# A two-block layer kernel on one core: the last expert's weights in another order and cut, and the last norm in two halves

## What is computed

```
probs = softmax(h @ w_router);  gate, idx = top_k(probs transposed, 64)   # 64 tokens per expert
xs = h[idx]
a = xs @ w_gate;  u = xs @ w_up             # [16, 64, 1024] x [16, 1024, 2048]
y = (silu(a) * u) @ w_down                  # [16, 64, 2048] x [16, 2048, 1024]
x = x + segment_sum(y * gate, idx)          # back to the 512 token rows
out = x * rsqrt(mean(x * x, columns) + 1e-6) * final_g
```

## Time and profile before

| | us |
|---|---|
| three runs, median | 2015.63 (2015.32 to 2016.61) |
| the profiled execution, its own time | 2017.26 |
| span of its trace, first to last instruction | 2015.9 |
| PE busy, of the span | 1843.2 (91%) |
| DVE busy | 594.0 (29%) |
| ACT busy | 284.5 (14%) |
| mean granted TensorE clock | 0.983 |
| moved by DMA | 589.86 MB |

### The profile page before, as it was taken

How to read it: one execution, slowest core, us unless ns; L and a number is a source line. 1 busy time by engine, 2 the same in 40 slices (tenths; PEclk the granted TensorE clock), 3 DMA queues, 4 the chain that set the end, 5 groups by cost and what they waited for, 6 DMA issues and landing times.

```text
span 2015.9 us, 20480 instructions
## 1 busy us (share of the span) xinstructions
PE 1843.2 (91%) x8850; PEld 842.5 (42%) x8850; DVE 594.0 (29%) x1103; ACT 284.5 (14%) x519; POOL 33.4 (2%) x44
## 2 busy tenths in 40 slices
PE   8999999999999989999998999888888889888886
PEld 4445788453333344567654333222222223222222
DVE  4478354341010147984323111111110111111112
ACT  3222100211101036231011000000000000000001
POOL 0000000010000010000000000000000000000000
PEclk9999999989999989999998999999999999999999
DMA  6221042369999942112458999999999999999996
GB/s 251 75 84 42 1 168 99 140 233 348 412 391 408 385 160 84 42 48 74 186 225 332 402 427 428 429 427 427 429 427 428 428 427 428 428 428 428 427 428 273
DMA packets 68542, 589.86 MB, mean 293 GB/s; under 512 B 5472, under 2 KB 6880, under 8 KB 37216
## 3 DMA queue, kind: packets, MB, share of 16 engines
q1 hardware_dynamic: 59904, 556.55, 67.1%
q10 hardware_dynamic: 4448, 17.28, 2.2%
q0 software_dynamic: 4096, 14.68, 2.1%
HBM read 575.91 MB, written 12.58 MB: 292 GB/s over the span
## 4 chain that ended last, share of the span: by engine, by line
PE 61%; DMA 32%; DVE 4%; issue 1%; ACT 1%; POOL 0%; ACTq 0%; DVEq 0%
PE ps L251 24%; DMA AR<-in_w_up 16%; PE ps L1241 11%; DMA AR<-in_w_down 9%; PE ps L2416 8%; DMA ring<-in_w_up 5%; PE ps L2442 5%; PE ps L787 3%; PE ps L2030 3%; PE ps L265 2%; PE ps L706 1%; PE ps L1920 1%; DMA ring<-in_exp_w_gate 1%; PE ps L2397 1%; PE ps L261 1%
## 5 line engine op out<-in xcount | busy, mean ns | idle before, releaser
L251 PE MATMUL ps<-AR,ring 128*128 128x512 f32 (+1 forms) x1160 | 383.1, 487 | 2.5 <-DVE AR L2246 2.4
L2556 DVE TENSOR_TENSOR XT<-XT,ps 128x512 f32<-128x512 f32 x128 | 81.9, 683 | 785.2 <-PE ps L2397 785.2
L251 PEld LDWEIGHTS ps<-AR,ring 128*128 128x128 f32 x1160 | 219.7, 190 | 155.8 <-issue 136.0
L2416 PE MATMUL ps<-ring,AR 128*64 128x512 f32 x1008 | 230.6, 601 | 48.4 <-DMA ring<-in_w_up 32.1
L2416 PE MATMUL ps<-AR 128*64 128x512 f32 x1040 | 235.5, 597 | 29.8 <-DMA AR<-in_w_up 23.8
L1241 PE MATMUL ps<-ring,AR 128*32 128x512 f32 x1536 | 249.5, 597 | 3.5 <-ACT AR L1389 1.9
L2416 PEld LDWEIGHTS ps<-ring,AR 128*64 128x64 f32 x1008 | 69.5, 137 | 201.9 <-issue 114.7
L2416 PEld LDWEIGHTS ps<-AR 128*64 128x64 f32 x1040 | 71.9, 137 | 189.5 <-issue 122.7
L251 PE MATMUL ps<-AR 128*128 128x256 f32 (+6 forms) x678 | 136.3, 346 | 6.7 <-DVE AR L1410 2.7
L1241 PE MATMUL ps<-AR 128*32 128x512 f32 x768 | 125.1, 595 | 0.0
L2442 PE MATMUL ps<-AR 128*64 128x512 f32 x528 | 117.9, 594 | 6.2 <-DMA AR<-in_w_down 6.2
(11 more groups left out here) (367 smaller groups left out, 1232.3 us busy)
## 6 DMA issues: line engine op xcount, KB each, us to landing
AR<-in_w_gate SPq DMA_DIRECT2D x33, 2048.0 KB, 35.0
AR<-in_w_down SPq DMA_DIRECT2D x33, 2048.0 KB, 35.4
ring<-in_w_up SPq DMA_DIRECT2D x32, 2048.0 KB, 35.4
AR<-in_w_up SPq DMA_DIRECT2D x32, 2048.0 KB, 35.0
ring<-in_w_gate SPq DMA_DIRECT2D x31, 2048.0 KB, 32.1
ring<-in_w_down SPq DMA_DIRECT2D x31, 2048.0 KB, 35.4
ring<-in_w_in SPq DMA_DIRECT2D x15, 2048.0 KB, 8.6
ring<-in_exp_w_gate SPq DMA_DIRECT2D x15, 2048.0 KB, 8.8
```

The lines of the kernel that those rows point to most:

```text
L251: x = PE.matmul(ps, l, r, start=i == 0, stop=i == len(pairs) - 1)
L2416: x = PE.matmul(GU[2 * m + f // 2][64 * (f % 2):64 * (f % 2) + 64, :], XS[n // 2 % 2][:, k * P + 64 * b:k * P + 64 * b + 64], w[:, kk_, f ...
L2556: DV.tensor_tensor(XK[:, o:o + T], XK[:, o:o + T], co_bank(i)[:, :], ALU.add).then_inc(d_co, 1)
```

## The change

Five edits, all at the last expert (number 15) and behind it.

1. The last expert's loads come as four gate parts, then four up parts, then the down parts; PE's loop follows. ACT's silu waits for the gate parts alone, and DVE waits for the up parts itself.
2. The last expert's down weights are cut by output columns: parts 0 and 1 hold columns 0 to 511 (1024 hidden rows each), parts 2 and 3 columns 512 to 1023. Each part is issued as two DMAs of 1 MB, whose contiguous runs are 2 KB. The second DMA of the last part has a semaphore of its own, so that PE can start on the first.
3. PE accumulates columns 0 to 511 in bank 4 and 512 to 1023 in bank 5. Even and odd hidden chunks go to the two partition halves, and the combine product with all 128 rows contracted adds the two. So there are 4 combine products of 128 rows for each column half: those of the first half stand between part 2 and part 3, those of the second after part 3. Eight banks are used so that few of them wait.
4. DVE adds the first column half, computes mean square/1024 + eps of it from ACT's sums, and multiplies the first half by `gn` while later work goes on. ACT squares the first half before it copies the second bank.
5. Behind the second half: ACT squares 512 columns of a row tile and takes the root with the first half's sum as bias; DVE takes the reciprocal and finishes the second half; ACT scales the first half by the reciprocal (`scaled`). The store of a tile waits for both. The last tile is stored as two halves, as before, the second column half first.

The diff, cut to this:

```diff
-        for e in range(16):
+        for e in range(15):
             ...
+        for m, (name, w) in enumerate((("cg", "w_gate_2"), ("cu", "w_up_2"))):
+            for c in range(4):
+                load(f"{name}15.{c}", runs(A[w][15], 256 * c, 2), e_gu, 120 + 4 * m + c + 1)
+        for c in range(4):
+            load(f"cd15.{c}", (A["w_down_2"][15][c % 2 * D:c % 2 * D + D, sl(c // 2)], 8 * T), e_dn, 60 + c + 1)
...
+            if n >= at["cd15.0"]:
+                for q in range(2):
+                    SP.dma_start(dst[:, sl(q, 4 * T)].rearrange("p (k n) -> p k n", k=4),
+                                 x.src[sl(q), :].rearrange("(p k) n -> p k n", k=4))\
+                        .then_inc(s_tail if q and n == at["cd15.3"] else s_ring[s], 16)
+                return
...
-            return CO[i % 2] if i < 120 else bank[(6, 7, 0, 1, 2, 3)[i % 8 % 6]]
+            return CO[i % 2] if i < 120 else bank[(0, 1, 2, 3, 6, 7, 4, 0)[i - 120]]
...
+            def combine_last(h):
+                PE.wait_ge(a_ye, 16 + h)
+                for a in range(4):
+                    i = 120 + 4 * h + a
+                    if i == 124:
+                        PE.wait_ge(d_co, 120)
+                    elif i == 127:
+                        PE.wait_ge(d_co, 121)
+                    PE.matmul(co_bank(i)[:, :], cGE[1][:, sl(a, P)], cYE[1 - h][:, :], start=True, stop=True).then_inc(e_co, 1)
+            def down_last():
+                for c in range(4):
+                    h, j = divmod(c, 2)
+                    w, s, v = weights(f"cd15.{c}", 8)
+                    PE.wait_ge(s, v + 16 if c < 3 else v)
+                    PE.wait_ge(a_hb, 31 + j)
+                    for q in range(2):
+                        if c == 3 and q:
+                            PE.wait_ge(s_tail, 16)
+                        for kk_ in range(4):
+                            g = kk_ % 2
+                            x = PE.matmul((DN, TR)[h][64 * g:64 * g + 64, :], cHB[1][:, 8 * j + 4 * q + kk_, :],
+                                          w[:, 4 * q + kk_, :], start=j == q == 0 and kk_ < 2, stop=j == q == 1 and kk_ > 1,
+                                          tile_position=(0, 64 * g), skip_group_check=True)
+                    x.then_inc(e_dn, 1)
+                    if c > 1:
+                        combine_last(c - 2)
...
-            for a in range(4):
-                combine(15, a)
...
-                    AC.wait_ge(e_gu, 8 * n + 8)
+                    AC.wait_ge(e_gu, 8 * n + 8 if n < 15 else 124)
...
-                AC.wait_ge(e_dn, 4 * n + 4)
+                AC.wait_ge(e_dn, 4 * n + 4 if n < 15 else 62)
...
+                AC.wait_ge(d_co, 121 + a)
+                AC.activation(SJ[a], XK[:, a * D:a * D + T], ACT.Square, accum_out=sx[:, a:a + 1]).then_inc(f_sd, 1)
+            AC.wait_ge(e_dn, 64)
+            AC.wait_ge(e_co, 120)
+            AC.activation(cYE[0], TR[:, :], ACT.Copy).then_inc(a_ye, 1)
+            def scaled(a):
+                x = XK[:, a * D:a * D + T]
+                AC.wait_ge(f_y, 2 * a + 1)
+                AC.activation(x, x, ACT.Copy, scale=rr[:, a:a + 1]).then_inc(f_sd, 1)
+            AC.wait_ge(s_cv, V3_GN)
+            for a in range(4):
+                AC.wait_ge(d_co, 125 + a)
+                AC.activation(SJ[4 + a], XK[:, a * D + T:a * D + D], ACT.Square, accum_out=sy[:, a:a + 1]).then_inc(f_sd, 1)
+                AC.wait_ge(f_sd, ROOTS[a] - 1)
+                AC.activation(rr[:, a:a + 1], sy[:, a:a + 1], ACT.Sqrt, bias=bx[:, a:a + 1], scale=1.0 / D).then_inc(f_sd, 1)
+                if a:
+                    scaled(a - 1)
+            scaled(3)
...
+                if n == 15:
+                    DV.wait_ge(e_gu, 128)
...
+            add_last(0)
+            DV.wait_ge(f_sd, 4)
+            DV.wait_ge(s_p3, 32)
+            DV.tensor_scalar(bx, sx, 1.0 / D, EPS, ALU.mult, ALU.add).then_inc(s_cv, 1)
             for a in range(4):
+                v = XK[:, sl(2 * a)]
+                v = DV.tensor_tensor(v, v, gn[:, 0:T], ALU.mult)
+            v.then_inc(s_cv, 1)
+            add_last(1)
+            for a in range(4):
+                DV.wait_ge(f_sd, ROOTS[a])
+                DV.reciprocal(rr[:, a:a + 1], rr[:, a:a + 1]).then_inc(f_y, 1)
                 DV.wait_ge(f_y, 2 * a + 1)
+                x = XK[:, sl(2 * a + 1)]
+                DV.scalar_tensor_tensor(x, x, rr[:, a:a + 1], gn[:, T:D], ALU.mult, ALU.mult).then_inc(f_y, 1)
...
                 SP.wait_ge(f_y, 2 * a + 2)
+                if a == 3:
+                    SP.dma_start(out[0, 3 * P:4 * P, T:D], XK[:, 3 * D + T:4 * D]).then_inc(s_out, 16)
+                SP.wait_ge(f_sd, SCALED[a])
                 n = D if a < 3 else T
                 SP.dma_start(out[0, a * P:(a + 1) * P, 0:n], XK[:, a * D:a * D + n]).then_inc(s_out, 16)
```

More of the change, by code:

```diff
@@ L129, in build @@
         s_out = sem("s_out")
-        s_dv, s_po = sem("s_dve_chain"), sem("s_pool_chain")
-        dv, po = Count(), Count()
+        s_tail = sem("s_tail")
+        s_dv = sem("s_dve_chain")
+        dv = Count()
         class Load:
@@ L2315, in build @@
         ss = area(4)
-        lg = area(64).rearrange("p (a n) -> p a n", a=4)
+        lgf = area(64)
+        lg = lgf.rearrange("p (a n) -> p a n", a=4)
         q4 = area(4).rearrange("p (a n) -> p a n", a=4)
@@ L2327, in build @@
         HK = [XG2[0], XS[0]]
+        sx, sy, bx, rr = (lgf[:, 4 * i:4 * i + 4] for i in range(4))
+        SJ = [v[:, sl(i)] for v in (XS[0], AR[:, X0 - 2 * D:X0 - D], AR[:, X0 - D:X0], XG2[0]) for i in range(2)]
+        ROOTS, SCALED = (6, 8, 11, 14), (9, 12, 15, 16)
         gatb, ixb, first_ = (scr[:, 256 + 64 * i:320 + 64 * i] for i in range(3))
@@ L2341, in build @@
         V2_LG, V2_PR, V2_SC, V2_IF, V2_IP, V2_ID = 1, 2, 3, 4, 5, 7
+        V3_BX, V3_GN = V2_ID + 1, V2_ID + 2
         e_tx, a_xs, d_ge, a_si, d_he, e_ht, a_hb, a_ye, e_co, d_co = (
@@ L2389, in combine @@
                     r = slice(64 * h, 64 * h + 64)
[L2390 to L2393, removed]
+                    if i >= 2:
                         PE.wait_ge(d_co, i - 1)
-                    elif a == 3:
-                        PE.wait_ge(d_co, i - 5)
                     PE.matmul(co_bank(i)[:, :], cGE[b][r, a * P:(a + 1) * P], cYE[b][r, :], start=True, stop=True,
                               tile_position=(64 * h, 0)).then_inc(e_co, 1)
+            def combine_last(h):
[24 more added lines that the diff above has]
+                        combine_last(c - 2)
             PE.wait_ge(s_cv, V2_ID)
@@ L2404, in pe_choice @@
                 b = n % 2
[L2405 to L2423, removed]
+                for i in range(8):
+                    c, m = divmod(i, 2) if n < 15 else (i % 4, i // 4)
+                    w, s, v = weights(f"{('cg', 'cu')[m]}{n}.{c}", 2)
+                    PE.wait_ge(s, v)
+                    if i == 0:
+                        PE.wait_ge(a_xs, 2 * (n // 2) + 2)
+                        if n:
+                            PE.wait_ge(d_he, 2 * n)
+                    for kk_ in range(2):
+                        k = 2 * c + kk_
+                        for f in range(4):
+                            x = PE.matmul(GU[2 * m + f // 2][64 * (f % 2):64 * (f % 2) + 64, :],
+                                          XS[n // 2 % 2][:, k * P + 64 * b:k * P + 64 * b + 64],
+                                          w[:, kk_, f * 512:(f + 1) * 512], start=k == 0, stop=k == 7,
+                                          tile_position=(0, 64 * (f % 2)), skip_group_check=True)
+                    x.then_inc(e_gu, 1)
+                    if n and i % 2:
+                        combine(n - 1, i // 2)
+                    if i == 3 and (n == 1 or b == 0 and 0 < n < 14):
                         rows(n // 2 + 1)
@@ L2431, in pe_choice @@
                     transposes(HB[f], [cHE[b][:, f * T + s:f * T + T:4] for s in range(4)]).then_inc(e_ht, 1)
+                if n == 15:
+                    down_last()
+                    break
                 for c in range(4):
@@ L2570, in dve_choice, with add_last @@
                     DV.tensor_tensor(cHE[b][:, sl(f)], cHE[b][:, sl(f)], GU[2 + f][:, :], ALU.mult).then_inc(d_he, 1)
-            def inverse(a):
-                DV.wait_ge(f_sd, 2 * a + 2)
-                DV.reciprocal(ss[:, a:a + 1], ss[:, a:a + 1]).then_inc(f_y, 1)
+            def add_last(h):
+                for a in range(4):
+                    x = XK[:, sl(2 * a + h)]
+                    DV.wait_ge(e_co, 121 + 4 * h + a)
+                    DV.tensor_tensor(x, x, co_bank(120 + 4 * h + a)[:, :], ALU.add).then_inc(d_co, 1)
+            DV.wait_ge(d_co, 120)
+            add_last(0)
+            DV.wait_ge(f_sd, 4)
+            DV.wait_ge(s_p3, 32)
+            DV.tensor_scalar(bx, sx, 1.0 / D, EPS, ALU.mult, ALU.add).then_inc(s_cv, 1)
             for a in range(4):
-                combine(15, a)
-            DV.wait_ge(s_p3, 32)
+                v = XK[:, sl(2 * a)]
```

(16 more changed lines are left out.)

## The result

The changed kernel took 2021.01 us in the median of 16 runs (2017.63 to 2023.06), the kernel before 2016.65 beside them (2014.41 to 2021.02). The ratio is 1.0016 with a 95% interval of 1.001 to 1.0022: slower by 3.2 us, between 2.0 and 4.4. Its middle is inside the 0.2% that I called no change, on its slow side; the interval reaches just beyond. (The two medians lie 4.4 us apart and the two means 3.9; I go by the ratio.) The profiled execution has a span of 2021.1 us against 2015.9.

What follows compares the result with a forecast made beforehand. Weight loads set the pace until the last down part; only the serial 18.6 us behind it could change. Combine and load wait +2.3, tail -0.4, sum +1.9 on a median of 2015.63: 2017.5 us, range 2014.9 to 2020.0.

Steps and rivals of the forecast that it cites:

- Edit 1: Last expert's gate parts before up parts: 0 us, the multiply staying behind two adds of the previous combine's last quarter.
- The cut loads: Last down parts in 2 KB runs: 5.42 us a part instead of 4.90, PE waiting 1.1 us for part 2.
- Rival 1: Last down loads: 2 KB runs cost nothing, so +0.75 us, 2016.4; chance 0.15.
- Rival 2: Wait for part 2: cut loads much slower, at least 6.1 us a part; 2021.8 at 306 GB/s; chance 0.08.
- The combine: Last expert's combine: four 128-row products take 3.63 us; the last add ends 2.3 us later.
- Rival 3: Last expert's combine: full-array products cost only 0.46 us each, so -1.4 us, 2014.2; chance 0.07.
- The norm's first half: First column half's squares and multiplies hidden before the second half's first add: 0 us, with 1.3 us of cover.
- The tail at -0.4: Behind the first reciprocal: the last store lands 7.85 us after it instead of 8.3, so -0.4 us.

Runs made afterwards that it cites:

- gate_first: The kernel before with only the last expert's gate parts put ahead of its up parts and the two waits split; ratio 0.9994 to the kernel before.
- wide_runs: The changed kernel with the last down parts read as contiguous 8 KB runs instead of 2 KB; ratio 1.0006 to the kernel before.
- short_combine: The changed kernel with the last expert's combine products over 64 rows on alternating row halves instead of 128; ratio 1.0003 to the kernel before.
- late_combine: The changed kernel with both column halves' combine behind part 3 and ACT's second bank copy before its squares; ratio 1.0026 to the kernel before.
- early_split2: The kernel before with gate before up, expert 14's last combine quarter earlier, last down part in three transfers, the one before in two; ratio 0.9988.
- early_split: The kernel before with gate before up, expert 14's last combine quarter before the last up part, last down part in three transfers; ratio 0.9987.
- after_again: The changed kernel run once more, unchanged; ratio 1.0015 to the kernel before.

## Why the prediction was right, point by point

The forecast was +1.9 us; measured is +3.2 (2.0 to 4.4), which on the forecast's base of 2015.63 is 2018.9, inside the range, and on the side of slower that the forecast named. The range was wide (2014.9 to 2020.0), and its width helped: the traces account for 2.3 to 2.5 us of the 3.2. By its steps:

- **Edit 1 at nothing**: right. The multiply is at L + 5.95 in the kernel before, in the changed one and in `gate_first`.
- **The cut loads**: right in size. Part 2 was awaited until L + 16.05, 5.35 us a part (forecast 5.42, and 4.90 without the cut). It cost 1.0 us (forecast 1.15), shown by `wide_runs`. Rival 1 falls with it. Rival 2 as well, by its own condition: it needed 6.1 us a part. The rate is a weaker argument than it looks. Until 1995 none of the stretches of about 5 us that I took was below 373 GB/s, but while the last part came in it was 201 (first trace of the changed kernel):

```profile
1990.00:1995.00 5.00, 5.00 (x24) 1.60 (x22) 0.00 (x0) 0.00 (x0) 0.00 (x0) 0.93 1.04 383
1995.00:2000.00 5.00, 5.00 (x26) 1.54 (x22) 0.00 (x0) 2.08 (x3) 0.00 (x0) 1.00 0.53 201
```

SP did stand, and nothing waited for it. One row holds six of its eight issues; the first of them took 22.53 us, the others 2.4 to 2.6 each:

```profile
1954.69 35.27 SPq L251 DMA_DIRECT2D AR<-in_w_down  x6
```

- **The combine**: right. From start to start 3.64 us for four products (forecast 3.63), the last add ends at L + 32.0 to 32.2 (forecast 32.2, before 29.9): +2.1 to +2.3. `short_combine` takes back 2.4 us and so shows it to be the largest term. Rival 3 falls.
- **The norm's first half at nothing**: right, with 1.36 us of cover left (forecast 1.3). `late_combine` shows what it costs without it.
- **The tail at -0.4**: wrong in sign. Behind the first reciprocal T the kernel before needs 8.3 us, the changed one 8.5. The step that failed is that the stores, once begun sooner, also end sooner. The third store went at T + 4.1 instead of T + 3.8, since ACT's scaling takes 0.72 us and not the 0.6 that I had put, and a round of square, root and scaling 1.55 us from store to store and not 1.5; and what came after it took 4.4 us to the end, not 4.05:

```profile
2014.37 0.71 ACT L2540 ACTIVATE XT<-XT,AR 128x512 f32<-128x512 f32 x1
```

DVE has two us less to do behind the last add, and the stores begin 0.5 us sooner after it. But between them the DMA engines now run half empty twice (rows of the first trace of the changed kernel; the emptiest such half us of the kernel before has about 0.78):

```profile
2015.50:2016.00 0.50, 0.00 (x0) 0.00 (x0) 0.00 (x0) 0.47 (x4) 0.00 (x0) 0.50 0.47 189
2017.00:2017.50 0.50, 0.00 (x0) 0.00 (x0) 0.00 (x0) 0.24 (x1) 0.00 (x0) 0.50 0.56 221
```

Read in steps of 0.05 us, the output's bytes move from T + 2.3 to T + 7.95 before and from T + 1.85 to T + 7.9 after, so almost all of the half us won at the front is gone at the end. Part of it goes in the gaps, the rest in one late piece. A store raises its semaphore sixteen times, and the span ends with the last of these. Fifteen of the last store's sixteen are there at T + 8.1 in both traces of the changed kernel, 0.2 us sooner than before, and the sixteenth at T + 8.4. It comes 0.30 to 0.33 us behind the fifteenth in all six traces with the new norm, and at most 0.05 behind it in five of the six with the old one (in `early_split2` 0.29). Why it is late, no run shows.

Sum of the traces: +2.1 to +2.3 and +0.2, that is 2.3 to 2.5 instead of 1.9.

**What stays open** is the rest to 3.2, and whether it is anything. If it is real, it lies before L. L is 1975.0 to 1979.9 in the six traces of kernels that hold the old order of the combine, and 1977.8 to 1981.3 in the six of the others, though up to L their work differs only in edit 1, which `gate_first` has too. The difference is there ahead of the first expert's products (start and count, in the chains of before and after):

```profile
1086.02 27.70 PE ps L2416 x128
```

```profile
1089.80 27.70 PE ps L2457 x128
```

In all twelve traces these products start at 1085.0 to 1088.4 in the six of the old order and at 1087.9 to 1089.8 in the six others.

Part of it comes with a slower clock in one stretch of the first block: from 404 to 412 us the granted clock is 0.63 to 0.68 in four of the twelve traces and 0.79 to 0.81 in eight, and the 16 products that begin there take 9.7 to 9.9 us against 8.4 to 8.7. But one of the four is `early_split`, of the first group. No experiment was made on it. The ratios of the five changed kernels with the old combine also lie about 0.06% below what their tails say, so part of it may be measurement.

## What to carry to other kernels

Before work is moved beside a wait, ask how long the wait is and what the moved form costs: here PE had 0.8 us of wait near the place, none of it before part 3, and got products that cost 3.6, because the way the result was cut took away the pairs of 64-row products that ran side by side. A partial sum that is cheap to make can be dear to use. When a stream of loads ends in a few us of work, cut the last transfers and let the work start on the first piece, and do it for each part that the engine still waits for, since closing one wait only shows the next. And once the output's own bytes fill the end, shortening the arithmetic ahead of them wins at most what it brings forward the first store, and only if the stores behind it still follow without gaps; here they did not, and nothing was won.

## What the runs showed of the hardware that I had not expected

While SP stood at issues of cut loads, one of 22.5 us and five of 2.4 to 2.6, the DMA engines stayed full (share 1.04). A third length of run fits between the two that I had: 8 KB gave 419 and 424 GB/s in two stretches, against 373 to 388 for 2 KB and 428 for 16 KB. ACT's copy with a scale from a register of each row took 0.72 us for 512 columns, against 0.60 for one from PSUM without.

What I had overlooked in both kernels is how the stream of loads ends. The last down part of the kernel before lands while the engines are half used:

```profile
1987.00:1998.00 11.00, 10.19 (x50) 3.81 (x47) 0.00 (x0) 0.00 (x0) 0.00 (x0) 1.00 0.53 223
```

The sixteen increments of its semaphore fall into two groups: eight by 1992.74, the other eight between 1995.08 and 1997.25, and PE starts at 1997.29. In `after_again` those of the last transfer are at 1995.25 to 1996.75 and at 1998.87 to 2001.22. So half of the transfer was there some 4.5 us ahead of the other half, and PE's wait goes by the slower one. If both halves could have ended together, the last part would have landed about 2.2 us earlier in the kernel before; that is an estimate, half of the 4.5 us between 1992.74 and 1997.25, and no run tried it.
